# First stage of a two-layer transformer kernel: conditioning rows in pairs, scaled tokens and the first three projection tiles column by column

## The reference

```python
cond = jax.nn.silu(c)
mod = cond @ w_ada[l] + b_ada[l]
sh1, sc1, g1, sh2, sc2, g2 = jnp.split(mod, 6, axis=-1)
h = modulate(rms_norm(x, norm_mix_g[l]), sh1, sc1)   # h * (1 + scale) + shift
proj = h @ w_in[l]
```

## Time and profile before

| | |
|---|---|
| median of 3 runs | 2065.77 us (2064.53 to 2066.44) |
| the profiled execution | 2062.07 us, its span 2060.3 us |
| mean granted TensorE clock | 0.989 |
| TensorE (PE) busy | 1967.4 us, 95% of the span |
| VectorE (DVE) busy | 1210.3 us, 59% |
| ScalarE (ACT) busy | 902.1 us, 44% |
| GpSimd (POOL) busy | 93.2 us, 5% |
| chain that ended last | PE 85%, DVE 7%, ACT 3%, DMA 2%, issue 2%, SP's queue 1% |

### The profile page before, as it was taken

One profiled execution on the slowest core, in us unless ns is written; L12 is line 12 of the kernel. 1 busy time (PEld: TensorE's weight loads), 2 busy tenths in 40 slices (PEclk: granted clock), 3 DMA queues, 4 the chain that ended last, 5 costly groups with the idle time before them and its releaser, 6 DMA issues.

```text
span 2060.3 us, 23855 instructions
## 1 busy us (share of the span) xinstructions
PE 1967.4 (95%) x8936; PEld 1527.7 (74%) x8936; DVE 1210.3 (59%) x1770; ACT 902.1 (44%) x1486; POOL 93.2 (5%) x172
## 2 busy tenths in 40 slices
PE   4999999999989989999999899999999999999897
PEld 2778876656687768888888688887887876776575
DVE  5686656655585787687555536647434454445645
ACT  4443245555563542333333325424524664445642
POOL 1001100000000000111000000000010000000000
PEclk9999999999999999999999999999999999999998
DMA  9335510010204523445221733344421010003043
GB/s 337 113 103 192 186 52 11 1 52 0 93 1 147 170 92 118 143 170 193 78 70 65 274 119 130 119 158 154 131 100 46 32 42 31 21 21 133 1 174 122
DMA packets 63200, 216.07 MB, mean 105 GB/s; under 512 B 6896, under 2 KB 8048, under 8 KB 62832
## 3 DMA queue, kind: packets, MB, share of 16 engines
q1 hardware_dynamic: 43472, 141.15, 20.2%
q0 software_dynamic: 19616, 73.41, 10.1%
HBM read 177.30 MB, written 34.60 MB: 103 GB/s over the span
## 4 chain that ended last, share of the span: by engine, by line
PE 85%; DVE 7%; ACT 3%; DMA 2%; issue 2%; SPq 1%; POOL 0%; DVEq 0%; ACTq 0%
PE ps L1142 14%; PE ps L1144 14%; PE ps L1143 14%; PE ps L1275 9%; PE ps L1431 6%; PE ps L1433 6%; PE ps L1432 6%; PE ps L1252 3%; PE ps L1253 2%; PE ps L1219 2%; DMA w_raw<-in_weights 1%; PE ps L1234 1%; DMA cmask<-in_consts 1%; SPq L2698 1%; PE ps L1222 1%
## 5 line engine op out<-in xcount | busy, mean ns | idle before, releaser
L1142 PE MATMUL ps<-h_hi,w_hi 128*128 128x512 f32 x832 | 335.8, 404 | 16.7 <-DVE h_lo L2058 10.1
L1144 PE MATMUL ps<-h_hi,w_lo 128*128 128x512 f32 x832 | 326.1, 392 | 0.0
L1143 PE MATMUL ps<-h_lo,w_hi 128*128 128x512 f32 x832 | 325.9, 392 | 0.0
L2021 DVE TENSOR_TENSOR w_lo<-w_raw,w_hi 128x1024 fp32r<-128x1024 f32 x139 | 170.0, 1224 | 251.1 <-ACT w_hi L1565 249.7
L1565 ACT ACTIVATE w_hi<-w_raw 128x1024 fp32r<-128x1024 f32 x140 | 147.7, 1056 | 264.2 <-DMA w_raw<-in_weights 262.4
L2149 DVE TENSOR_REDUCE mh<-ps 128x1 f32<-128x512 f32 x192 | 124.7, 654 | 147.6 <-PE ps L1219 70.7
L1142 PEld LDWEIGHTS ps<-h_hi,w_hi 128*128 128x128 f32 x832 | 157.8, 190 | 54.7 <-issue 12.0
L1144 PEld LDWEIGHTS ps<-h_hi,w_lo 128*128 128x128 f32 x832 | 157.1, 189 | 34.1
L1143 PEld LDWEIGHTS ps<-h_lo,w_hi 128*128 128x128 f32 x832 | 157.7, 189 | 31.6 <-issue 1.4
L1142 PE MATMUL ps<-hid_hi,w_hi 128*128 128x512 f32 x352 | 139.3, 396 | 6.8 <-DVE hid_late_lo L2021 2.9
L1431 PE MATMUL ps<-t_hi,pair_S_r 128*128 128x512 f32 x352 | 137.8, 391 | 3.5 <-DVE pair_S_r L2021 2.6
(11 more groups left out here) (384 smaller groups left out, 3849.7 us busy)
## 6 DMA issues: line engine op xcount, KB each, us to landing
w_raw<-in_weights SPq DMA_DIRECT2D x140, 512.0 KB, 3.6
ada_next<-in_ada POOLq DMA_DIRECT2D x32, 512.0 KB, 4.6
ada_last<-in_ada POOLq DMA_DIRECT2D x24, 512.0 KB, 5.5
pair_gate<-in_weights SPq DMA_DIRECT2D x22, 512.0 KB, 3.7
pair_up<-in_weights SPq DMA_DIRECT2D x22, 512.0 KB, 4.7
ada_first<-in_ada SPq DMA_DIRECT2D x8, 1024.0 KB, 14.9
m_scratch<-y POOLq DMA_DIRECT2D x12, 512.0 KB, 5.0
hid_scratch<-hid_out POOLq DMA_DIRECT2D x22, 256.0 KB, 2.3
```

The costliest lines, as they stand in the source:

```text
L1142: e.matmul(o, w_hi[slot][:, tile_of(kw)], hi, start=start, stop=False, skip_group_check=skip)
L1143: e.matmul(o, w_hi[slot][:, tile_of(kw)], lo, start=False, stop=False, skip_group_check=skip)
L1144: return e.matmul(o, w_lo[slot][:, tile_of(kw)], hi, start=False, stop=stop, skip_group_check=skip)
L2021: return e.tensor_tensor(dst, src, hi.bitcast(F32), ALU.subtract)
```

## The change

The first stage is written as a list of its own, `first_tiles`. Conditioning row k (a shift) and row 8 + k (its scale) come in one transfer and are reduced one after the other, and step `mods` makes the scale of that one column. As soon as columns are ready they are scaled for half 0 (`hw` and `hlo`, which are the parts of the former `h`) and multiplied with the weight tiles 0, 1, 2. The sum of squares and the root of half 1 stand behind the first four columns of half 0. SP's loads are put in that order, x's half 0 first. In half 1 tiles 0 and 1 go column by column in turn, and tile 2 follows in portions as before.

```diff
     fill = portions("proj", "y1", IN1_ORDER, IN1_ORDER.index, True)
+    for i in range(15):
+        fill[i] = [x for x in fill[i] if not (x[0] == "proj" or x[0] == "y1" and i < 12)]
...
+def first_tiles(p):
...
+    def rows(*ks):
+        for k in ks:
+            add(("ada", k), ("ada", 8 + k), ("mods", k))
+
+    def h(n, *ks):
+        for i, k in enumerate(ks):
+            p.add("hw", n, k)
+            if i:
+                p.add("hlo", n, ks[i - 1])
+        p.add("hlo", n, ks[-1])
+
+    def products(n, tiles, *ks):
+        for k in ks:
+            add(*[("first", IN1_ORDER[t], n, k) for t in tiles])
+
+    add(("xsq", 0), ("xr", 0))
+    rows(0, 1)
+    h(0, 0, 1)
+    p.add("w", 0)
+    products(0, (0,), 0, 1)
+    rows(2)
+    p.add("w", 1)
+    products(0, (1,), 0, 1)
+    rows(3)
+    h(0, 2, 3)
+    p.add("w", 2)
+    products(0, (0, 1), 2, 3)
+    products(0, (2,), 0, 1, 2, 3)
+    add(("xsq", 1), ("xr", 1))
+    rows(4, 5)
+    h(0, 4, 5)
+    products(0, (0, 1, 2), 4, 5)
+    rows(6, 7)
+    h(0, 6, 7)
+    products(0, (0, 1, 2), 6, 7)
+    p.add("mod1")
+    h(1, 0, 1, 2, 3)
+    add(*[("y1", t, 0) for t in IN1_ORDER[:3]])
+    h(1, 4, 5, 6, 7)
+    products(1, (0, 1), *range(KT))
...
+            def first_tile(t, n, k):
+                i, bank = IN1_ORDER.index(t), proj_bank(no("y1", t, n))
+                if n == 0 and k == 0:
+                    e.wait_ge(s["w_lo"], w_no("w", i))
+                e.wait_ge(s["h_lo"], KT * n + k + 1)
+                x = three(ps[:, bank, :], i % 3, k, h_hi[:, k, half_of(n)], h_lo[:, k, half_of(n)], k == 0, k == KT - 1)
...
-            def h(n):
-                if n == 0:
+            def h(n, k):
+                if n and k == KT - 1:
                     e.wait_ge(s["masks_made"], 5)
...
+            def mod_tile(k):
+                e.wait_ge(s["ada_done"], 2 * k + 2)
+                e.scalar_tensor_tensor(s_mix[:, k:k + 1], mod1[:, 8 + k:9 + k], 1.0, col("norm_mix_g", k), ALU.add, ALU.mult).then_inc(s["scale_made"], 1)
...
+                def rows(k):
+                    if k >= 6:
+                        e.wait_ge(s["ada_done"], 2 * (k - 5))
...
+                half(0)
+                rows(0)
+                rows(1)
                 load_weights(0)
-                rows(14)
+                rows(2)
+                load_weights(1)
+                rows(3)
+                load_weights(2)
+                half(1)
+                for k in range(4, 8):
+                    rows(k)
```

More of the change, by code:

```diff
@@ L599, in network, with add @@
     second_block(p, between(1))
+def first_tiles(p):
+    def add(*steps):
+        for step in steps:
+            p.add(*step)
+    def rows(*ks):
[35 more added lines that the diff above has]
+    products(1, (0, 1), *range(KT))
 def schedule():
@@ L605, in schedule @@
     p.add("ada_rows")
[L606 to L616, removed]
+    first_tiles(p)
     first_block(p)
@@ L1552, in y_norm @@
                 e.matmul(ps[:, 2 + n, :], ones[:, :], sq3[1][:, :], start=False, stop=True).then_inc(s["norm_mm"], 1)
-            work = {"xsq": x_squares, "proj": proj, "rsum": head_squares, "vprep": vprep, "max": max_unit,
+            work = {"xsq": x_squares, "first": first_tile, "proj": proj, "rsum": head_squares, "vprep": vprep, "max": max_unit,
                     "mrow": mrow, "sc": scores, "val": values, "gate": gate, "mk": m_keys, "mv": m_values, "mm": m_decays,
@@ L1600, in xr @@
                 inverse_root(norm_no("xr", n), 4 + n, rstd[n])
-            def h(n):
-                if n == 0:
+            def h(n, k):
+                if n and k == KT - 1:
                     e.wait_ge(s["masks_made"], 5)
-                for k in range(KT):
-                    e.wait_ge(s["h_pre"], KT * n + k + 1)
-                    e.activation(h_hi[:, k, half_of(n)], wide[k % 4][:, :], ACT.Identity, bias=mod1[:, k:k + 1]).then_inc(s["h_hi"], 1)
+                e.wait_ge(s["h_pre"], KT * n + k + 1)
+                e.activation(h_hi[:, k, half_of(n)], wide[k % 4][:, :], ACT.Identity, bias=mod1[:, k:k + 1]).then_inc(s["h_hi"], 1)
             def y_out(t, n):
@@ L2000, in y_norm @@
                 inverse_root(norm_no("yr", n), 2 + n, rs3[n])
-            work = {"start": start, "cond": lambda: condition(1), "w": round_weights, "xsq": x_squares, "xr": xr, "h": h, "y1": y_out, "silu": silu, "rtab": exp_tables,
+            work = {"start": start, "cond": lambda: condition(1), "w": round_weights, "xsq": x_squares, "xr": xr, "hw": h, "y1": y_out, "silu": silu, "rtab": exp_tables,
                     "rsq": head_squares, "rln": head_roots, "attend": attend, "khi": k_high, "qhi": q_high, "mrow": mrow, "sc": scores, "take": take,
@@ L2049, in mod_first, with h_wide, h_low @@
             def mod_first():
-                e.wait_ge(s["ada_done"], 16)
-                scale_col(s_mix, "norm_mix_g", mod1, 8).then_inc(s["scale_made"], 1)
                 e.memset(xp_two[1][:, 0:2], 0.0).then_inc(s["pad_made"], 1)
                 e.memset(xp_two[1][:, 2 + T:4 + T], 0.0).then_inc(s["pad_made"], 1)
[L2055 to L2061, removed]
-                e.wait_ge(s["norm_r"], n + 1)
[L2063 to L2070, removed]
+            def mod_tile(k):
+                e.wait_ge(s["ada_done"], 2 * k + 2)
+                e.scalar_tensor_tensor(s_mix[:, k:k + 1], mod1[:, 8 + k:9 + k], 1.0, col("norm_mix_g", k), ALU.add, ALU.mult).then_inc(s["scale_made"], 1)
+            def h_wide(n, k):
+                e.wait_ge(s["scale_made"], k + 1)
+                e.wait_ge(s["norm_r"], n + 1)
+                if KT * n + k >= 4:
+                    e.wait_ge(s["h_lo"], KT * n + k - 3)
+                e.scalar_tensor_tensor(wide[k % 4][:, :], xt[:, k, half_of(n)], s_mix[:, k:k + 1], rstd[n][:, :], ALU.mult,
+                                       ALU.mult).then_inc(s["h_pre"], 1)
+            def h_low(n, k):
+                e.wait_ge(s["h_hi"], KT * n + k + 1)
+                e.scalar_tensor_tensor(h_lo[:, k, half_of(n)], wide[k % 4][:, :], mod1[:, k:k + 1], h_hi[:, k, half_of(n)].bitcast(F32),
+                                       ALU.add, ALU.subtract).then_inc(s["h_lo"], 1)
             def conv(t):
@@ L2695, in first_rows, with half @@
             def first_rows():
[L2697 to L2702, removed]
+                def rows(k):
+                    if k >= 6:
+                        e.wait_ge(s["ada_done"], 2 * (k - 5))
+                    e.dma_start(ada_first[4 * (k % 2) + k // 2][:, :, :], a["ada"][k:k + 9:8].rearrange("o p d -> p o d")).then_inc(ada_place(k)[1], 16)
+                def half(n):
                     e.dma_start(xt[:, :, half_of(n)], a["x"][:, :, half_of(n)].rearrange("k p t -> p k t")).then_inc(s[f"x_in{n}"], 16)
-                for o in range(8, 14, 2):
-                    rows(o)
+                half(0)
+                rows(0)
+                rows(1)
                 load_weights(0)
-                rows(14)
+                rows(2)
[5 more added lines that the diff above has]
+                    rows(k)
                 e.dma_start(cmask[:, :, :], a["consts"][3:8].rearrange("n p c -> p n c")).then_inc(s["mask_in"], 16)
@@ L2803, in end @@
                     e.wait_ge(s[f"out{n}"], 64)
-            work = {"start": start, "w": lambda i: load_weights(i) if i else None, "ada_rows": first_rows, "gl": load_pair, "back": back,
+            work = {"start": start, "w": lambda i: load_weights(i) if i >= 3 else None, "ada_rows": first_rows, "gl": load_pair, "back": back,
                     "gate": gate, "wout": wout, "down": down, "angle": angle, "swap": swap,
```

15 lines of the change are left out of this document (8 added, 7 removed).

## The result

| | median | runs | profiled execution | its span | mean clock |
|---|---|---|---|---|---|
| changed kernel | 2069.82 us (2065.16 to 2073.49) | 20 | 2072.19 us | 2070.4 us | 0.983 |
| kernel before, beside it | 2064.53 us (2058.64 to 2066.95) | 20 | 2062.07 us | 2060.3 us | 0.989 |

The ratio is 1.0026, with a 95% interval of 1.0018 to 1.0034: the change makes the kernel slower, by 5.3 us of 2065. The forecast was no change, 2065.2 us, and the result lies just outside its range.

The account below looks back on a forecast made before the run. Loads were taken to hold up the start and TensorE to set the time from 56 us; the first product of tile 2, half 1 comes 0.6 us earlier, the rest costs nothing: 2065.77 - 0.6 = 2065.2 us, range 2061.5 to 2069.5.

Parts of the forecast that it names:

- The bound and the loads: Start: loads hold it up before the change; reordered at 2.65 us per MB, none late for VectorE afterwards.
- Root of half 0: Start: the root of x's half 0 is ready at 24.6 us, VectorE idling 4 us for it.
- The clock in the start: TensorE's rise to the high clock, taken at 40.6 us, the middle between 37.75 and 43.5.
- the early end: Clock already high from 37.75 us: root of half 1 at 51.1, first product of tile 2, half 1 at 75.7 (-2.5).
- The new wait: VectorE stands at column 4's low part from 46.4 to 53.7 us, for ScalarE behind half 1's root.
- M1: Marker, first product of tile 2, half 1: forecast at 77.6 us instead of 78.17, 0.6 earlier.
- The clock falls in the gap before column 6: Rival: TensorE's clock falls while idle from about 58.2 to 62.5 us, +2.3 us, 2068.1; chance 0.15.
- The start follows the loads: Rival: the last conditioning pair, landing at 43.0 us, sets the start; 16.9 us early, 2048.9; chance 0.05.
- slower: the clock stays low until the sum is over: Rival: TensorE at low clock until half 1's sum of squares ends; +9.4 us, 2075.2; chance 0.05.
- The change does what it says: Against the rival that VectorE's chain from 24.6 us runs longer than added; no chance of its own.
- Behind the marker: After tile 2, half 1's first product: tile 3's weights covered by some 4 us, costed at nothing; uncovered, at most 5.2.

Follow-up runs that it names:

- a_look3: Changed kernel, unaltered, one more single run for a third profile; first product of tile 3, half 0 at 89.42 us, no median given.
- a_look4: Changed kernel, unaltered, one more single run for a fourth profile; first product of tile 3, half 0 at 90.77 us, no median given.
- a_rsq_early: Changed kernel with the first head norm's square on ScalarE ahead of rounding weights 3 and 4; 2065.02 us, 0.9997 of the kernel before.
- a_tilewise: Changed kernel with half 1 of tile 0 over all columns first, then tile 1; 2069.31 us, 1.0024 of the kernel before.
- three: Changed kernel with the square early, half 1's sum and root behind columns 4 and 5, conditioning pair 2 reduced earlier; 2055.21 us, 0.9949 of before.
- four: Like three, but half 1's squares back ahead of columns 4 and 5, only the root behind them; 2054.19 us, 0.9952 of the kernel before.
- a_sum_later: Changed kernel with half 1's sum and root behind the scaling of columns 4 and 5 of half 0; 2067.57 us, 1.0008 of before.

## Why the prediction was wrong

- **The bound and the loads**: right. VectorE waits for no conditioning row behind 20 us, and the last pair is reduced as soon as VectorE gets to it.
- **Root of half 0**: 24.3 against 24.6. Right.
- **The clock in the start**: its rise was taken at 40.6 and came at about 32.5 in the profiled execution (products follow each other at 0.43 at 29.4 and at 0.23 at 32.9), the early end that I had named. The sum starts at 42.99 instead of 44.55. In a_look3 it rose only at 40.1, near the middle.
- **The new wait**: 5.9 us against 7.3, for that same reason. Right in kind.
- **M1**: 76.12, 75.99, 76.66, 78.68 against 77.6, all within the ends 75.7 and 79.0. Right, and the mean gains 1.3 us, not 0.6. But the early end was added up wrongly: 24 products at 0.228 from 37.75, 7.1 for the sum and 1.35 for the root give 51.7, not 51.1, so that end of the marker is 76.3, not 75.7, and two of the four came 0.2 to 0.3 us ahead of it.
- **The clock falls in the gap before column 6**: it fell at the gap before column 4 instead, in or up to 1.2 us behind 2.84 us of idle time, in the profiled execution and two more, and at both gaps, before columns 4 and 6, in a_look4. In the profiled execution it costs nothing: TensorE waits 2.27 us at column 6 all the same, and what it does late it does in that gap. At column 6 of a_look4 it costs 1.5 us, where the rival said 2.9. That a gap of 4.3 us "should just hold" was read off one row, and the gaps of 2.84 us and of 2.21 (column 6 of a_look4) did not hold. The low clock at 52.7 to 56.1 is also one of the signs that I had named for being wrong (low beyond 46 us).
- **The start follows the loads**, **slower: the clock stays low until the sum is over**: neither. The sum took 7.03 us, at full clock. The changed kernel was slower for a reason that no rival of mine had.
- **The change does what it says**: yes.
- **Behind the marker: the step that failed.** It followed the weights of tile 3 to TensorE, found them covered, and left the head sum at its wait of 1.36. Weights 3 were covered indeed. But the place of the head sum, 5.6 us behind the marker, was carried over from the kernel before as if it were fixed. It hung on the square, which stands behind weights 4 on ScalarE, and neither their landing nor the queue ahead of their rounding was worked out anew. With the two half tiles ending together, weights 4 land 4.8 to 5.5 us after their issue instead of 3.3, and the first landing stands ahead of rounding, copy, rounding and square; the two end within 0.3 us of each other in all four executions. In the profiled one the square ends at M1 + 7.3. The head sum waits 3.1 to 3.7, and the clock falls at the end of that wait. The term costed at nothing measured 3.4 us in the profiled execution, and 3.5 as the mean of four (12.4 from M1 to M2 instead of 8.9); a_rsq_early takes it out, and the time is that of the kernel before.

**What the Trainium skill's rule made of it.** The advice on all K tiles of one output tile before a wait ("TensorE: Matmul & The Clock Gate", section on HAM oscillation), which the page gives for thin-M matmuls that wait for DMA, spoke against this order, and the result has its sign. The clock did fall in a wait between columns here (2.84 us), at no cost in the profiled execution. a_tilewise follows it for tiles 0 and 1 of half 1 and is no faster, 1.0024, and three and four, column by column, are the fastest of all. The order of columns by itself is not the cause; the ready square behind the two late loads is.

**What stays open.** Of the 5.3 us (4.1 in the second comparison) 2.3 are at M2 on the mean of four executions, 1.4 in the profiled one. The other 2 to 3 lie behind M2, where the instructions are the same. The medians less M2 in the table vary by as much among kernels with no difference there, so it may be the scatter of M2 and of the clock behind it. The runs don't settle whether the later M2 also makes the clock fall more often. Nor do they tell the queue on ScalarE from the late landing of weights 4: no run changes one and leaves the other.

## What to carry to other kernels

When a change makes two tiles end together instead of one after the other, go through each in-order engine's queue behind the later marker, and add up what now stands behind the first late transfer: a transfer that is itself covered can still hold up a small step behind it that is not. Don't carry a landing time over either: here two loads asked for within 0.7 us both landed later than one alone. Put such a step ahead of the instruction that waits for the transfer. And carry a marker's gain as far as the next wait of the bounding engine before you count it.

## What the runs showed of the hardware

**TensorE's clock falls after short gaps, and not in each execution.** I had taken the fall 5.3 us after work ended as the time that a gap must last. The same place of the program, a wait for `w_lo`, in the changed kernel, TensorE in order of time:

```profile
727.05 0.50 PE L1185 MATMUL ps<-h_hi,w_hi 128*128 128x512 f32 x1 [1.76 <-DVE w_lo L2070]
```

The stretches behind it, busy time by engine, with the clock third from the end:

```profile
728.60:732.00 3.40, 3.40 (x10) 2.66 (x9) 2.83 (x4) 1.65 (x2) 0.00 (x0) 0.50 0.65 242
732.00:736.00 4.00, 4.00 (x19) 3.28 (x18) 2.44 (x5) 1.51 (x3) 0.00 (x0) 1.00 0.10 25
```

The kernel before there, TensorE in order of time:

```profile
722.67 0.50 PE L1142 MATMUL ps<-h_hi,w_hi 128*128 128x512 f32 x1 [1.72 <-DVE w_lo L2021]
```

and its stretch behind it:

```profile
724.40:727.80 3.40, 3.40 (x16) 2.82 (x15) 2.95 (x5) 1.66 (x2) 0.00 (x0) 1.00 0.61 235
```

A gap of 1.76 us is followed by 3.4 us at 1.2 GHz, with 10 matmuls in place of 16, one of 1.72 at the same place by none. Such a stretch costs half its length, some 1.7 us of full-speed work. Behind M2 the clock records of the changed kernel's profiled execution hold 56.9 us at 1.2 GHz and those of its repetition 37.2; half of the difference is 9.9 us, and the one takes 1982.0 us from M2 on and the other 1972.6. In the other two executions it is 49.4 us with 1977.8 from M2 on, and 34.1 with 1972.6. The 20 runs of the changed kernel spread by some 4 us to either side, about as much as this change is worth; that these stretches make the spread is argued from the four profiles, not shown.

**Two weight loads issued together land later each.** In a_tilewise the two loads (512 KB each) are issued 5.5 us apart, and ScalarE's rounding starts 3.5 and 3.4 us behind the copies; the conditioning row issued 0.46 us behind the first of them did not slow it. In the changed kernel they are issued 0.7 us apart, with a conditioning row 0.9 us ahead of them in three of the four executions and 2.5 in a_look4. The rounding of weights 3 starts 4.2, 4.5, 5.0 and 4.3 us behind the copy, and weights 4 land 5.1, 5.1, 5.5 and 4.8 us after their issue. In a_sum_later the first takes 5.9 us and the second 6.4. What makes it 4.2 in one execution and 5.9 in another the runs don't show.
